# Layer 1's condition vectors 8 to 10: weighted rows on VectorE, summed over the partitions by TensorE

## What is computed

```python
c_act = jax.nn.silu(c)
for layer in range(DEPTH):
    mod = c_act @ w_ada[layer] + b_ada[layer]
    sh1, sc1, g1, sh2, sc2, g2 = jnp.split(mod[:, None, :], 6, axis=-1)
    h = rmsnorm(x, mix_norm_g[layer]) * (1.0 + sc1) + sh1
    ...
    x = x + g1 * y
    h = rmsnorm(x, ffn_norm_g[layer]) * (1.0 + sc2) + sh2
    x = x + g2 * hierarchical_moe(h, ...)
```

## Time and profile before

| | us |
|---|---|
| median of three runs | 1291.33 |
| the three runs | 1290.84 to 1291.56 |
| time of the profiled execution | 1292.23 |
| its span | 1290.1 |

### The profile page before, as it was taken

How to read it: one execution, slowest core, us unless ns; L and a number is a source line. 1 busy time by engine, 2 the same in 40 slices (tenths; PEclk the granted TensorE clock), 3 DMA queues, 4 the chain that set the end, 5 groups by cost and what they waited for, 6 DMA issues and landing times.

```text
span 1290.1 us, 14421 instructions
## 1 busy us (share of the span) xinstructions
PE 914.9 (71%) x5948; PEld 445.8 (35%) x5948; DVE 328.2 (25%) x874; ACT 159.0 (12%) x393; POOL 18.3 (1%) x66
## 2 busy tenths in 40 slices
PE   4999899565656466485779999985655747556647
PEld 2866444221212121221358655531212223121213
DVE  1287436111120211111131044622111111112022
ACT  1013311000000000000123245210000000000000
POOL 1000100000000000000000000000000000000000
PEclk8899899797887787887899999987878778787789
DMA  9976949999999999999996358599999999999996
GB/s 364 391 306 252 408 165 414 429 428 428 427 428 428 427 428 428 429 427 427 414 408 261 131 199 324 221 416 427 428 428 427 428 427 429 429 427 428 428 423 254
DMA packets 60584, 490.05 MB, mean 380 GB/s; under 512 B 7649, under 2 KB 8050, under 8 KB 38002
## 3 DMA queue, kind: packets, MB, share of 16 engines
q1 hardware_dynamic: 58048, 486.62, 90.8%
q10 hardware_dynamic: 2482, 2.64, 0.6%
HBM read 488.20 MB, written 1.05 MB: 379 GB/s over the span
## 4 chain that ended last, share of the span: by engine, by line
DMA 51%; PE 42%; SPq 2%; DVE 2%; issue 1%; ACT 1%; POOL 0%; ACTq 0%; DVEq 0%
PE psum L1333 42%; DMA weight_ring<-in_moe_w_up 18%; DMA weight_ring<-in_moe_w_down 16%; DMA weight_ring<-in_moe_w_gate 13%; DMA weight_ring<-in_w_ada 4%; SPq L426 2%; PE psum L1390 1%; DVE phase_region L1292 0%; PE psum L1847 0%; DVE phase_region L1318 0%; ACT phase_region L614 0%; ACT phase_region L755 0%; DVE phase_region L991 0%; POOL phase_region L558 0%; DVE x_tokens L1142 0%
## 5 line engine op out<-in xcount | busy, mean ns | idle before, releaser
L1333 PE MATMUL psum<-weight_ring,phase_region 128*32 128x512 f32 (+1 forms) x3584 | 464.7, 681 | 333.3 <-DMA weight_ring<-in_moe_w_gate 146.6
L1333 PEld LDWEIGHTS psum<-weight_ring,phase_region 128*32 128x32 f32 x3584 | 137.0, 129 | 644.8 <-issue 619.0
L1333 PE MATMUL psum<-phase_region 128*128 128x128 f32 (+6 forms) x880 | 162.7, 347 | 4.7 <-DVE x_tokens L1142 1.7
L1333 PEld LDWEIGHTS psum<-phase_region 128*128 128x128 f32 (+2 forms) x880 | 105.5, 190 | 77.6 <-issue 57.2
L1333 PE MATMUL psum<-h_or_mix_T,weight_ring 128*128 128x256 f32 (+1 forms) x520 | 116.5, 384 | 5.0 <-ACT h_or_mix_T L642 3.2
L1333 PEld LDWEIGHTS psum<-h_or_mix_T,weight_ring 128*128 128x128 f32 x520 | 100.0, 196 | 19.4 <-DMA weight_ring<-in_even_w_in 3.7
L1333 PE MATMUL psum<-weight_ring,h_or_mix_T 128*128 128x512 f32 x224 | 101.4, 604 | 3.4 <-DVE scale L886 3.4
L1201 DVE TENSOR_TENSOR phase_region<-psum,gate_rows 128x512 f32<-128x512 f32 x32 | 22.1, 692 | 235.2 <-PE psum L1333 235.2
L1194 DVE SCALAR_TENSOR_TENSOR phase_region<-phase_region,psum 128x512 f32<-128x512 f32 x16 | 16.9, 1056 | 221.9 <-PE psum L1333 221.9
L1189 DVE SCALAR_TENSOR_TENSOR phase_region<-phase_region,psum 128x512 f32<-128x512 f32 x16 | 11.0, 688 | 244.6 <-ACT phase_region L764 244.6
L755 ACT ACTIVATE phase_region<-psum,shift,scale 128x128 f32<-128x128 f32 x72 | 27.1, 456 | 361.8 <-PE psum L1333 361.8
(11 more groups left out here) (189 smaller groups left out, 427.0 us busy)
## 6 DMA issues: line engine op xcount, KB each, us to landing
weight_ring<-in_moe_w_gate SPq DMA_DIRECT2D x64, 2048.0 KB, 22.1
weight_ring<-in_moe_w_up SPq DMA_DIRECT2D x64, 2048.0 KB, 20.1
weight_ring<-in_moe_w_down SPq DMA_DIRECT2D x64, 2048.0 KB, 20.3
weight_ring<-in_w_ada SPq DMA_DIRECT2D x12, 3072.0 KB, 14.8
weight_ring<-in_w_ada SPq DMA_DIRECT2D x12, 1024.0 KB, 16.9
weight_ring<-in_odd_w_in SPq DMA_DIRECT2D x6, 2048.0 KB, 25.3
weight_ring<-in_even_w_in SPq DMA_DIRECT2D x4, 2048.0 KB, 19.0
weight_ring<-in_even_w_out SPq DMA_DIRECT2D x2, 2048.0 KB, 11.7
```

Of the source, the lines that this page charges most:

```text
L1333: return pe.matmul(out_, lhsT, rhs, start=first, stop=last, **kw)
```

## The change

- VectorE forms, for the slabs of vectors 8, 9 and 10, the weighted row sum in place: row k of the slab (1024 columns) times that partition's condition value, added to `ROWS`, for k = 0 to 7, each step behind the one before (`weigh`). `ROWS` is the whole of the tile `ada_partials`, one buffer for all three vectors.
- Vector 8's eight steps stand one behind each of the outputs u = 3 to 10. Vector 9's steps 0, 1, 2 stand behind u = 13, 14, 15 and the other five behind that; vector 10's stand four before and four behind `biased(1)`.
- TensorE's `add_rows` sums `ROWS` over the partitions with a matrix of ones: two matmuls of 512 columns for vector 8 before projection 13, which gives all partitions the result, so the join is gone; four matmuls of 256 columns for vector 9 before projection 18 and for vector 10 in head 0.
- `take_modulation` of 8, 9, 10 moves to behind u = 12, behind `biased(0)` and into head 1. ScalarE's copy for vector 8 is gone. SyncE's waits for the places of 8, 9 and 10 are now on `ada_weighted`.

```diff
@@ ring @@
         def ada(n, at):
+            if n in WEIGHTED:
+                return ("ada", n, at, ada_weighted, WEIGHTED.index(n) + 1)
             return ("ada", n, at, ada_summed, sums_by(n))
@@ scalar @@
-                if h == 0:
-                    copy_partials(fills1[h])
@@ vector @@
+            def weigh(n, lo, hi):
+
+                s = slab_index("ada", n)
+                for k in range(lo, hi):
+                    if k == 0:
+                        dve.wait_ge(slab_in[SPOT[s]], landed(s))
+                        if n == 9:
+                            dve.wait_ge(ada_joined, 3)
+                        if n == 10:
+                            dve.wait_ge(ada_summed, sums_by(9))
+                        ins = v.tensor_scalar(ROWS, wide(s)[:, k, :], CCOL[:, 1, k:k + 1], None, ALU.mult)
+                    else:
+                        if k == ADA_FIRST:
+                            dve.wait_ge(rest_in[SPOT[s]], landed(s))
+                        dve.wait_ge(weight_step, weighted[0])
+                        ins = v.scalar_tensor_tensor(out=ROWS, in0=wide(s)[:, k, :], scalar=CCOL[:, 1, k:k + 1], in1=ROWS,
+                                                     op0=ALU.mult, op1=ALU.add)
...
+                if 3 <= u < 11:
+                    weigh(8, u - 3, u - 2)
+                if u == 12:
+                    take_modulation(8)
+                if u > 12:
+                    weigh(9, u - 13, u - 12)
...
+            weigh(9, 3, KD)
             biased(0)
+            take_modulation(9)
+            weigh(10, 0, 4)
             biased(1)
+            weigh(10, 4, KD)
...
-                if h - 1 in fills1:
-                    take_modulation(fills1[h - 1])
+                if h == 1:
+                    take_modulation(10)
@@ tensor @@
+            def add_rows(n):
+
+                pe.wait_ge(ada_weighted, WEIGHTED.index(n) + 1)
+                if n == 8:
+                    for half in range(2):
+                        ins = mm(PS[:, 6 + half, :], ONES[:, :], ROWS[:, half * HALF:(half + 1) * HALF], True, True)
+                    ins.then_inc(ada_joined, 1)
+                else:
+                    pe.wait_ge(qk_rstd, 16)
+                    for g in range(4):
+                        ins = mm(PS[32 * g:32 * g + 32, ADA_BANK[n], 0:256], ONES[:, 0:32], ROWS[:, 256 * g:256 * g + 256],
+                                 True, True, skip_group_check=True)
                     ins.then_inc(ada_summed, 1)
...
+                if u == 13:
+                    add_rows(8)
+                if u == 16:
+                    pe.wait_ge(ada_ready, 9)
+                if u == 18:
+                    add_rows(9)
...
-                if h in fills1:
-                    modulation_sums(fills1[h])
+                if h == 0:
+                    add_rows(10)
...
-                if h == 0:
-                    gate_join(fills1[h])
```

More of the change, by code:

```diff
@@ L82, in build_trunk @@
         PART = sb("ada_partials", [P, 4, 256])
+        ROWS = PART[:, :, :].rearrange("p g n -> p (g n)")
         SHIFT = sb("shift", [P, 4, KD])
@@ L206, in build_trunk @@
         ada_summed = sem("ada_summed")
+        ada_weighted = sem("ada_weighted")
+        weight_step = sem("weight_step")
         ada_copied = sem("ada_copied")
@@ L302, in build_trunk @@
         fills = {0: 3, 1: 4}
[L303 to L308, removed]
+        ADA_ORDER = (0, 1, 2, 6, 3, 7, 4, 5, 9, 10, 11)
+        WEIGHTED = (8, 9, 10)
+        ADA_BANK = (4, 5, 4, 5, 5, 4, 5, 4, 7, 4, 5, 5)
+        COPIED = (2, 6, 7, 5, 11)
+        PART_SLOT = {2: 0, 6: 2, 7: 3, 5: 1, 11: 1}
         ADA_HEAD = ADA_ORDER[:8]
@@ L1275, in _ @@
             link(v.tensor_scalar(LAM[:, 5:6], LAM[:, 4:5], -LAM0, None, ALU.add))
+            weighted = [0]
+            def weigh(n, lo, hi):
[14 more added lines that the diff above has]
+                                                     op0=ALU.mult, op1=ALU.add)
+                    if k < KD - 1:
+                        weighted[0] += 1
+                        ins.then_inc(weight_step, 1)
+                    else:
+                        ins.then_inc(ada_weighted, 1)
             for u in range(16):
@@ L1347, in modulation_sums @@
                     slab_ready(s)
-                    if n in (0, 8):
-                        pe.wait_ge(cond_in_place, 1 + n // 8)
+                    if n in (0, 11):
+                        pe.wait_ge(cond_in_place, 1 + n // 11)
                     if n in (3, 5):
@@ L1352, in modulation_sums @@
                     elif n > 1:
-                        pe.wait_ge(ada_ready, {2: 1, 6: 2, 7: 3, 4: 4, 8: 8, 9: 8, 10: 9, 11: 10}[n])
+                        pe.wait_ge(ada_ready, {2: 1, 6: 2, 7: 3, 4: 4, 11: 11}[n])
                 cond = CREP if n in ADA_HEAD else CREP1
@@ L1361, in modulation_sums @@
                 if hi == KD:
+                    ins.then_inc(ada_summed, 1)
+            def add_rows(n):
[4 more added lines that the diff above has]
+                    ins.then_inc(ada_joined, 1)
+                else:
+                    pe.wait_ge(qk_rstd, 16)
+                    for g in range(4):
+                        ins = mm(PS[32 * g:32 * g + 32, ADA_BANK[n], 0:256], ONES[:, 0:32], ROWS[:, 256 * g:256 * g + 256],
+                                 True, True, skip_group_check=True)
                     ins.then_inc(ada_summed, 1)
```

## The result

| | before | changed |
|---|---|---|
| median | 1291.13 us (6 runs, 1290.45 to 1293.43) | 1296.34 us (6 runs, 1295.59 to 1299.28) |
| span of the profiled execution | 1290.1 us | 1294.1 us |
| first up weights issued | 819.59 | 823.68 |

The changed kernel takes 1.0041 times as long [1.0028, 1.0054], that is 3.6 to 7.0 us more, slower by more than the 0.2% that a measurement tells. The forecast was 1293.8 us, range 1290.3 to 1297.3. The two profiled spans differ by 4.0 us, within the interval.

The account below looks back on a forecast made before the run. TensorE's progress from 664 to 819.59 was taken to bound the kernel. Work won and lost came to -0.1 us, GpSimd made it +0.3, clock falls added 2.2: +2.5 on 1291.33, so 1293.8 us, range 1290.3 to 1297.3.

Parts of the forecast that it names:

- the exchange: Layer 1 up to head 4: VectorE's lateness against TensorE work removed, sum -0.1 us.
- the clock: Thin heads 0 to 2: TensorE's granted clock falls one to two times, 2.2 us, bounds 0 and 5.
- What bounds the kernel: TensorE from 664 to 819.59 sets when the last weight stream starts; after that everything shifts as one.
- Rival (d): Restart at 819.59 doesn't follow TensorE, or slabs of vectors 9 and 10 come late; 1291 us, chance 0.05.
- Vector 8: Behind outputs 3 to 10: its eight VectorE steps hide, by 1.0 us; its two matmuls cost TensorE 1.7.
- The waits of the line: TensorE waits for VectorE's steps, 1.4 us before projection 18 and 1.4 before head 0, which starts 5.0 late.
- The step, 1.25: Each VectorE weighting step over 1024 columns takes 1.25 us, 1.23 plus 0.03 between steps; floor 1.07.
- Rival (c): A VectorE step costs over 1.25 us; at 1.5, +2.5, and with the clock 1296.3 us; chance 0.15.
- What is won back: Heads 0 to 2 take 15.2 us instead of 19.9, periods set by VectorE and ScalarE: 4.7 won, not 9.9.
- GpSimd: Its biases beside VectorE's steps of vectors 9 and 10 delay them, from nothing to 1.5 us; 0.4 taken.
- rival (a): Heads 0 to 2 keep full clock through their gaps: +0.3 us, 1291.6 us, chance 0.27.

Follow-up runs that it names:

- short sums: The kernel before, with TensorE's sums of vectors 8, 9 and 10 over rows 0 and 7 only: 1289.89 us, ratio 0.9983.
- early and busy: The changed kernel with VectorE's steps of vectors 9 and 10 moved earlier and four useless matmuls in each of heads 0 to 2: 1290.17 us, 0.9993.
- vector 8 only: The changed kernel with only vector 8 weighted on VectorE; 9 and 10 summed whole by TensorE in heads 1 and 2: 1293.30 us, ratio 1.0007.
- fill with 10: The changed kernel with vector 9's steps earlier and vector 10's sums on TensorE, 12, 12 and 8 matmuls in heads 0 to 2: 1289.62 us, 0.9983.
- biases later: The changed kernel with GpSimd's biases held until vector 9's steps, and head 3's until vector 10's, are done: 1296.37 us, one run.
- steps early: The changed kernel with vector 9's steps two, five and one behind outputs 13 to 15 and five of vector 10 before `biased(1)`: 1292.28 us, 1.0011.

## Why the prediction came out as it did

The mechanism and nearly all places held; the size fell short, +2.5 forecast, +4.1 in the stage and +5.2 between the medians (3.6 to 7.0). The missing 1.6 in the stage are two terms of the sum, 0.8 in the exchange and 0.8 in the clock. The direction is that of the central figure only: the chances gave "same" 0.50 and "slower" 0.44, so the outcome was not the one held most likely.

- **What bounds the kernel**: held. 4.09 later at the restart, 4.0 in the span, the last stage unchanged. Rival (d) is out. One reading there was wrong without effect: the DMA isn't nearly empty ahead of the restart, its share from 784.00 to 819.59 is 0.45.
- **Vector 8**: held. Its eight steps hide, the adding starts at 714.65 without a wait and costs 1.72 (716.37 is the next row's start), forecast 1.7.
- **The waits of the line**: right in place, 2.01 and 1.36 against twice 1.4; head 0 late by 5.89 against 5.0 and 0.4 for GpSimd.
- **The step, 1.25**: the first of the two mis-sized terms. A step lasts 1.28 and the next starts 1.33 after it, so ten steps cost 0.8 more. The price came from L956, a TENSOR_TENSOR of 1.23. The right form stood in the same group: SCALAR_TENSOR_TENSOR takes 0.478 at 256 columns, and 1.28 at 1024 is that plus 0.80 for 768 columns. Rival (c) is what happened, at 0.08 a step.
- **What is won back**: periods 4.75 and 5.35, then 5.31 wherever the clock held, against 4.7, 5.2, 5.2 and 5.25. The exchange was to end at -0.1 and with GpSimd at +0.3; with the clock held it measured +1.07. Of the 0.8 between, 0.5 lies ahead of head 0 and 0.3 in the heads, which take 20.72 to head 4 and not 20.4. Ahead of head 0 the ten steps cost 0.8 more, and the probabilities of head 0 take about 0.3 less, since their two-column operation no longer has a bias beside it (0.23 instead of 0.51).
- **GpSimd**: 0.35 measured, 0.4 taken. The Trainium skill (SBUF — State Buffer, "Who interferes with whom") has a VectorE instruction with two SBUF inputs and a GpSimd instruction that reads SBUF exclude each other, the one that issues later being blocked for the whole of the other. The trace agrees in part: two biases take 2.92 instead of 0.99, so GpSimd is held up. But three biases, 1.5 us when alone, cost VectorE's line only 0.35, far from the +1.4 that the prediction set as that rule's end of the sum. And the row at 750.97 that the prediction put beside the rule has one tensor input and a scalar, not two tensor inputs.
- **The clock**: the second mis-sized term, 3.02 measured, 2.2 taken, two falls of 1.5 instead of one to two. The prediction took the row at 139.42 for thin work, and it isn't: ahead of that gap of 2.13 TensorE was busy for 8.08 us without a pause (first line below, the kernel before). Nor does the length of a gap decide by itself: one of 2.01 before projection 18, between dense pieces, left the clock at 1.00 (second line, the changed kernel), while in the thin heads the falls came within 1.5 us of gaps of 1.98 and 1.99.

```profile
129.21:137.29 8.08, 8.08 (x80) 4.62 (x80) 5.23 (x13) 1.22 (x2) 2.06 (x8) 0.79 1.02 407
...
742.00:750.00 8.00, 5.99 (x27) 2.72 (x27) 7.69 (x18) 2.45 (x9) 0.51 (x1) 1.00 0.01 2
```

The forecast of a fall thus came out right on a row that didn't show what it was read for, which is luck in part. What the runs show is that filled heads keep the clock, in four kernels of four, while short sums, with a pause of 1.80 in head 0, lost it. The fillings shorten the pauses too, so no run tells thin work as such from pauses that follow each other, or from the instant at which a pause comes. The Trainium skill (TensorE: Matmul & The Clock Gate, "What's actually happening") ties the low clock to idleness; read as one idle stretch it would have given rival (a), 1291.6. The trace speaks against that reading: in the heads TensorE was not idle for longer than 1.98 us ahead of the first fall, less than the 2.01 that it had passed at full clock.

Left over: between the medians lie 5.2 us, in the stage 4.1. That difference is inside the interval, and its cause stays open. Nor do the medians of the experiments follow the stage to a us (early and busy: -2.4 in the stage, -0.9 [-2.1, +0.4] in the median). The clock has other low stretches that differ between the profiled executions. One, at the start of layer 1, reaches into the projections in three of the ten kernels (changed, vector 8 only, short sums): from the first projection to the adding they take 51.9 to 52.2, the other seven 50.1 to 50.2. It lies ahead of the stage compared here. Another lies near 830:

```profile
830.00:834.00 4.00, 4.00 (x18) 3.26 (x17) 2.38 (x12) 0.00 (x0) 0.00 (x0) 0.57 0.94 389
```

That is fill with 10, behind its first up weights; seven kernels have such a stretch, and before, changed and biases later have none. Why it comes there was not tried.

## What to carry to other kernels

Work taken off the busiest engine is worth only what the others let through: find the period of the loop without it, from when the next input was ready and not from when it was used. A filling can also be what holds TensorE's clock, so remove it in parts and spread the rest over the thin places. Price an operation by a row of its own form, fixed part and slope, above all where ten of them stand in one line.

## What the chip showed that I had not expected

- The clock falls at the end of the thin place, and what follows pays for it: after one thin head of 4.7 us with a gap of 2.50, the following dense head took 9.04 us instead of 6.06.
- Adding 6 us of useless matmuls made the heads 3.0 us shorter. Real work cut into the same gaps kept the clock too (TensorE busy 16.20 of 20.67 us).
- Low stretches in the heads lasted 3.4 us (772.3 to 775.7, changed kernel) or 6.8 us (763.1 to 769.9, vector 8 only; twice in steps early). Biases later had one of each. Which one comes was not settled.
- A pause of 2.01 us between dense pieces left the clock at full speed, one of 1.98 in a thin head was followed by a fall within 1.5 us, and so was one of 2.13 that had dense work on both sides.
- VectorE beside GpSimd lost 0.24 of 8.19 us, while GpSimd's two operations grew from 0.99 to 2.92.
